# Even output projection of a two-layer trunk: eight products of halves against seven

## What is computed

```python
def even_layer(x, norm_g, w_in, conv_w, pool_w, pool_scale, w_out):
    h = rmsnorm(x, norm_g)
    xa, bg, cg, gate_a, u, gate_b = split_cols(h @ w_in, EVEN_SIZES)      # six parts of 512
    ya = short_conv_mixer(xa, bg, cg, conv_w) * jax.nn.silu(gate_a)
    yb = pool_mixer(u, pool_w, pool_scale) * jax.nn.silu(gate_b)
    return x + jnp.concatenate([ya, yb], axis=-1) @ w_out                # 1024 x 1024
```

## Time and profile before

| | |
|---|---|
| median of three runs | 1697.89 us (1697.84 to 1700.63) |
| profiled execution, its own time | 1699.45 us |
| profiled execution, its span | 1697.6 us |
| TensorE busy | 1673.1 us, 8096 matmuls |
| VectorE, ScalarE, GpSimd busy | 765.5, 483.3, 335.7 us |
| DMA over the span | 342.69 MB, mean 202 GB/s |

### The profile page before, as it was taken

One profiled execution on the slowest core, in us unless ns is written; L12 is line 12 of the kernel. 1 busy time (PEld: TensorE's weight loads), 2 busy tenths in 40 slices (PEclk: granted clock), 3 DMA queues, 4 the chain that ended last, 5 costly groups with the idle time before them and its releaser, 6 DMA issues.

```text
span 1697.6 us, 21999 instructions
## 1 busy us (share of the span) xinstructions
PE 1673.1 (99%) x8096; PEld 1391.4 (82%) x8096; DVE 765.5 (45%) x1328; ACT 483.3 (28%) x1153; POOL 335.7 (20%) x463
## 2 busy tenths in 40 slices
PE   8999999999999999999999999999999999999998
PEld 7887788888788788888888888888888888888886
DVE  3645335675422432566432333357544232245742
ACT  2000223562200023365310002437431000243731
POOL 8777674447400000000110000000001000000000
PEclk9999999999999999999999999999999999999999
DMA  8887687658855545544676555644467555554444
GB/s 270 308 292 263 217 287 237 208 182 286 310 195 191 179 168 195 166 134 140 229 256 198 187 183 177 194 141 137 145 228 265 192 189 183 186 172 141 136 161 149
DMA packets 162323, 342.69 MB, mean 202 GB/s; under 512 B 32128, under 2 KB 83840, under 8 KB 162208
## 3 DMA queue, kind: packets, MB, share of 16 engines
q1 hardware_dynamic: 139520, 313.57, 55.2%
q10 hardware_dynamic: 22688, 27.64, 5.2%
HBM read 263.50 MB, written 77.66 MB: 201 GB/s over the span
## 4 chain that ended last, share of the span: by engine, by line
PE 91%; DVE 3%; POOL 2%; ACT 1%; DMA 1%; issue 1%; ACTq 0%; POOLq 0%; DVEq 0%; SPq 0%
PE bank L478 14%; PE bank L480 14%; PE bank L479 14%; PE pair_a L478 5%; PE pair_a L480 5%; PE pair_a L479 5%; PE pair_b L478 4%; PE pair_c L478 4%; PE pair_c L480 4%; PE pair_c L479 4%; PE pair_b L480 4%; PE pair_b L479 4%; PE pair_a L773 2%; PE pair_c L756 2%; PE pair_b L670 1%; POOL slot L428 1%
## 5 line engine op out<-in xcount | busy, mean ns | idle before, releaser
L478 PE MATMUL bank<-h_hi,slot 128*128 128x512 f32 (+1 forms) x976 | 381.3, 391 | 5.1 <-POOL slot L428 2.1
L480 PE MATMUL bank<-h_hi,slot 128*128 128x512 f32 (+1 forms) x976 | 377.7, 387 | 0.0
L479 PE MATMUL bank<-h_lo,slot 128*128 128x512 f32 (+1 forms) x976 | 377.2, 387 | 0.0
L403 POOL TENSOR_TENSOR rs<-sums,eps 128x1 f32<-128x1 f32 x48 | 10.0, 207 | 1064.0 <-ACT junk L853 1064.0
L478 PEld LDWEIGHTS bank<-h_hi,slot 128*128 128x128 f32 x976 | 183.8, 188 | 43.6 <-POOL slot L428 2.3
L480 PEld LDWEIGHTS bank<-h_hi,slot 128*128 128x128 f32 x976 | 183.8, 188 | 37.8
L479 PEld LDWEIGHTS bank<-h_lo,slot 128*128 128x128 f32 x976 | 183.9, 188 | 37.2 <-issue 1.0
L428 POOL TENSOR_TENSOR slot<-stages,slot 128x512 fp32r<-128x512 f32 x132 | 180.6, 1368 | 11.0
L426 POOL TENSOR_SCALAR slot<-stages 128x512 fp32r<-128x512 f32 x132 | 93.2, 706 | 122.1 <-issue 104.5
L478 PE MATMUL pair_a<-h_hi,slot 128*128 128x512 f32 x256 | 101.3, 396 | 0.0
L480 PE MATMUL pair_a<-h_hi,slot 128*128 128x512 f32 x256 | 99.6, 389 | 0.0
(11 more groups left out here) (287 smaller groups left out, 3175.5 us busy)
## 6 DMA issues: line engine op xcount, KB each, us to landing
slot<-split_weights SPq DMA_DIRECT2D x396, 512.0 KB, 3.4
split_weights<-slot SPq DMA_DIRECT2D x132, 512.0 KB, 4.1
stages<-in_even_w_in SPq DMA_DIRECT2D x48, 256.0 KB, 3.8
stages<-in_odd_w_in SPq DMA_DIRECT2D x36, 256.0 KB, 3.2
result<-res ACTq DMA_DIRECT2D x16, 512.0 KB, 5.6
xin<-in_x ACTq DMA_DIRECT2D x12, 512.0 KB, 7.5
stages<-in_even_w_out SPq DMA_DIRECT2D x16, 256.0 KB, 3.2
stages<-in_odd_w_in SPq DMA_DIRECT2D x32, 128.0 KB, 2.8
```

The source lines that it names most:

```text
L478: t.matmul(dst, l_hi, r_hi, start=start, stop=False)
L479: t.matmul(dst, l_hi, r_lo, start=False, stop=False)
L480: return t.matmul(dst, l_lo, r_hi, start=False, stop=stop)
```

## The change

In blocks two to four (b = 1 to 3) the projection Y W (Y: 512 tokens x 1024, W: 1024 x 1024) is computed from halves. Y is cut by tokens (early, late: 256 each) and by rows of y (the convolution part and the pooling part, 512 each); W by rows and columns. Seven products of such halves take the place of eight. Four of them take sums of weight halves, three take stored halves; four take sums of y halves.

* PE: `seven_products` in place of the old order (now `plain_projection`, kept for block one). A product has four k-slices, each on one half unit and two token tiles: 6 matmuls. Order: P1, P2, P5, P6, P3, P4, the transposes of tile 0, P7 tile by tile with the transposes of tile 1 between, then the values. A block reads 28 half units there in place of 16 (`EXTRA` = 12).
* DVE: in blocks two to four the convolution's y stays in `res`; only the early half of it is split. After each `pool_end` four linked operations make the sums of y. The low parts of the sums (`sum_lo`) and 22 additions of 128x512 in place of 8 follow.
* ACT: high parts of the sums, and copies of the two banks of P1.
* GpSimd, in block two only: `combine(k)` makes four sums of weight slices and splits them in high and low. SP loads the raw slices, stores the results in `combined_weights` and reads them like other half units.
* The blocks two and three are written out on PE and SP instead of looped; on ACT and DVE block one now stands apart from the loop.

```diff
+HALVES1 = HALVES + EXTRA
+PRODUCTS = P1, P2, P5, P6, P3, P4, P7 = range(7)
+SUM1, SUM2, SUM4, SUM3 = range(4)
+ODD_BANK = (2, 0, 2, 0)
...
+            def save_combined(n):
+                sp.wait_ge(s_comb_split, n + 1)
+                sp.dma_start(combined_dram[n % 4, n // 4], combined[n % 2].bitcast(F32)).then_inc(s_comb_saved[n % 2], 16)
+                if n + 4 < 16:
+                    load_raw(n % 4, n // 4 + 1)
...
+            for place in range(4):
+                load_raw(place, 0)
+            for b in range(1, NB):
+                for i in range(HALVES1):
+                    if b == 1 and i >= 4 and i % 2 == 0 and i < 36:
+                        save_combined((i - 4) // 2)
+                    if b == 1 and i == 40:
+                        for place in range(2):
+                            sp.wait_ge(s_comb_saved[place], 16 * 8)
+                    if b < NB - 1 or i + SLOTS < HALVES1:
+                        sp.wait_ge(s_half, b * HALVES1 - EXTRA + i + 1)
+                        load_half((i + SLOTS) % HALVES1)
...
+            def combine(k):
...
+                g.tensor_tensor(stage[T1], stage[T3], stage[T1], ALU.subtract).then_inc(s_combined, 1)
...
+                for place in range(4):
+                    m = n + place
+                    if m >= 2:
+                        pool.wait_ge(s_comb_saved[m % 2], 16 * (m // 2))
+                    c_hi, c_lo = combined[m % 2][:, 0:HALF], combined[m % 2][:, HALF:2 * HALF]
+                    g.tensor_scalar(c_hi, stage[place], 1.0, 0.0, ALU.mult, ALU.add).then_inc(s_comb_hi, 1)
+                    pool.wait_ge(s_comb_hi, m + 1)
+                    g.tensor_tensor(c_lo, stage[place], c_hi.bitcast(F32), ALU.subtract).then_inc(s_comb_split, 1)
...
+                def seven_products():
+
+                    pe.wait_ge(s_pool_gate, b * 4 + 3)
+                    for k in range(4):
+                        product_of_y(P1, 0, 0, 0, k)
+                        if k == 0:
+                            pool_product(3)
+                    for k in range(4):
+                        if k == 0:
+                            pe.wait_ge(s_ye, b * 8 + 6)
+                        elif k >= 2:
+                            pe.wait_ge(s_ye, b * 8 + 4 + k + 1)
+                        product_of_y(P2, 4, 0, 4, k)
+                    product_of_sum(P5, SUM1, 6)
+                    pe.wait_ge(s_pool_gate, b * 4 + 4)
+                    product_of_sum(P6, SUM2, 2)
+                    pe.wait_ge(s_res, b * 8 + 2)
+                    product_of_sum(P3, SUM4, 4)
+                    pe.wait_ge(s_twelve, (b - 1) * 4 + 2)
+                    for k in range(4):
+                        product_of_y(P4, 4, 2 * P, 0, k)
+                    pe.wait_ge(s_res, b * 8 + 4)
+                    transposes(tile(0), 0, first_bank=ODD_BANK[0])
...
+                    for kp, tt in ((0, 0), (0, 1), (1, 0), (1, 1), (0, 2), (1, 2), (0, 3), (1, 3)):
+                        if kp == 0:
+                            pe.wait_ge(s_hlo, 2 * tile(tt) + 2)
+                        value_part(kp, tt)
+                        if tt == 1:
+                            if kp == 0:
+                                pe.wait_ge(s_res, b * 8 + 8)
+                            else:
+                                pe.wait_ge(s_hlo, 2 * tile(1) + 2)
+                            transposes(tile(kp + 2), kp + 2, first_bank=ODD_BANK[kp + 2])
...
+                    if not opening_block(b):
+                        early, late = y[:, 0:2 * P], y[:, 2 * P:TB]
+                        a11, a21, sum1, sum2 = [sums4[:, g, i, :] for i in range(4)]
+                        link(v.tensor_tensor(sum1, a21, late, ALU.add))
+                        link(v.tensor_tensor(sum2, sum1, a11, ALU.subtract))
+                        link(v.tensor_tensor(a11, a11, a21, ALU.subtract))
+                        v.tensor_tensor(a21, early, sum2, ALU.subtract).then_inc(s_sums, 1)
                     split_y(4 + g, y, s_ye)
```

More of the change, by code:

```diff
@@ L51 @@
 HALVES = 2 * UNITS
+EXTRA = 12
+HALVES1 = HALVES + EXTRA
 STAGES = 5
@@ L134, in trunk @@
         work = sb("work", [P, 8 * TB])
+        sums4 = res[:, :, :].rearrange("p k (s t) -> p k s t", s=4)
+        total = [work[:, 2048 + 512 * i:2560 + 512 * i] for i in range(2)]
         q_att = [y_hi, y_lo]
@@ L140, in trunk @@
         keys = sb("keys", [P, 2, KVH, KW], F32R)
+        combined = [keys[:, :, :, :].rearrange("p a g w -> p (a g w)")[:, 2 * HALF * i:2 * HALF * (i + 1)]
+                    for i in range(2)]
         k_hh = [keys[:, 0, g, :] for g in range(KVH)]
@@ L224, in trunk @@
         s_slot = [sem(f"slot_loaded{i}") for i in range(SLOTS)]
+        s_raw = [sem(f"raw_weights{i}") for i in range(4)]
+        s_combined = sem("weights_combined")
+        s_comb_hi = sem("combined_hi")
+        s_comb_split = sem("combined_split")
+        s_comb_saved = [sem(f"combined_saved{i}") for i in range(2)]
+        s_sums = sem("sums_of_y")
+        s_sum_step = sem("sum_step")
+        s_sum_hi = sem("sum_hi")
+        s_sum_lo = sem("sum_lo")
+        s_part = sem("partial_residual")
+        s_first_product = sem("first_product_copied")
+        s_twelve = sem("products_summed")
+        s_seven = sem("first_tile_of_p7")
         s_x = [sem(f"x_in{i}") for i in range(TT)]
@@ L332, in load_half, with load_raw @@
             def load_half(i):
-                sp.dma_start(slots[i % SLOTS][:, :].bitcast(F32), split_dram[i]).then_inc(s_slot[i % SLOTS], 16)
+                sp.dma_start(slots[i % SLOTS][:, :].bitcast(F32), later[i]).then_inc(s_slot[i % SLOTS], 16)
+            def load_raw(place, k):
+                col = {T1: 0, T3: HALF, T2: HALF, T4: 0}[place]
+                row = P * k + (HALF if place in (T2, T4) else 0)
+                sp.dma_start(stage[place], ewo[row:row + P, col:col + HALF]).then_inc(s_raw[place], 16)
+            def save_combined(n):
[3 more added lines that the diff above has]
+                    load_raw(n % 4, n // 4 + 1)
             x_rows = x[0]
@@ L601, in tile @@
                     return b * 8 + TT + tt
[L603 to L623, removed]
@@ L638, in body, with product_part, product_of_y @@
                             last.then_inc(s_half, 1)
-                    if kp == 0 and tt < 2:
-                        odd_transposes(tt + 2)
+                def product_part(p, k, t2, src_hi, src_lo, row, col, dst):
+                    sl, a = (2 * U_EOUT + 4 * p + k) % SLOTS, slice(col + t2 * P, col + (t2 + 1) * P)
+                    return mm3(banks[dst + t2], src_hi[:, row, a], src_lo[:, row, a], w_hi[sl], w_lo[sl],
+                               k == 0, k == 3)
+                def product_of_y(p, rows, col, dst, k):
+                    slot(2 * U_EOUT + 4 * p + k)
+                    for t2 in range(2):
+                        last = product_part(p, k, t2, y_hi, y_lo, rows + k, col, dst)
+                    last.then_inc(s_half, 1)
@@ L821, in _ @@
             body(0, True, False)
-            with pe.Fori(1, NB - 1) as b:
+            for b in range(1, NB - 1):
                 body(b, False, False)
```

314 lines of the change are left out of this document (248 added, 66 removed).

## The result

The change makes the kernel slightly slower: a median of 1702.1 us against 1698.0 us over 20 runs each, ratio 1.0022 (95% interval 1.0015 to 1.0028). The forecast was 1682.6 us. A second set of runs beside the last experiments gives 1703.8 against 1699.1 us, ratio 1.0025 (1.0014 to 1.0036).

What follows compares the result with a forecast made beforehand. TensorE was taken as the bound, busy 1673.1 of 1697.6 us. 72 fewer matmuls (-16.3 us) plus 1.0 for transposes gave -15.3: 1684.1 us against the profiled execution, 1682.6 us as median; 8 in 10 range 1681 to 1690.

Steps and rivals of the forecast that it cites:

- The stages: Projections of blocks two to four: 24 matmuls fewer each at 0.227 us, 16.3 us less in all.
- The weight traffic: Projection stages: 28 loads in place of 16, 512 KB every 1.36 us, 385 GB/s demanded; cost 0 us.
- The rival of late loads in the stage: The 28 loads of each of three stages land late, up to 9.9 us: +18 us, 1716 us; chance 7%.
- Row groups 5 and 6: Earlier trace rows for weight traffic: 408 to 416 GB/s with full queues; loads landing in 3.1 to 3.5 us in the stage.
- The chain of y and its sums: DVE after each pool end: four linked 128x256 operations, 1.65 us, done 2.7 us before PE wants them; 0 us.
- The transposes of tile 2: After P7, PE waits 0.6 us for DVE where it waited 0.28: +0.3 us a block, +1.0 us over three.
- Block two alone: GpSimd's weight sums and SP's raw loads and stores in block two: 0 us, at worst a few us once.
- SP is held up in block two: Rival: GpSimd's rounds 4 us longer hold SP's queue, PE waits 3 to 5 us once, 1687 us; chance 7%.
- catches up: Block two: SP, about 6 us late, recovers within a round, 21 us of work against 8 halves, 21.8 us.
- 3 us to spare: Opening of block two, where loads land in 5.8 to 9.9 us: ordinary loads still 3 us ahead of need.
- The range: Whole kernel: 8 in 10 range of the forecast time, 1681 to 1690 us.
- the held queue: Block two: SP's wait for GpSimd delays the ordinary loads behind it; forecast as a rival at 1687 us, chance 7%.

Runs made afterwards that it cites:

- experiment 3: The change with GpSimd issuing the 16 raw loads and 16 stores on its own queue: 1681.4 us, ratio 0.9899; again 1682.9 us, 0.9898.
- Experiment 7: The change with SP's ordinary load issued before the wait for GpSimd, store and raw load at 16 places: 1698.6 us, ratio 0.9998.
- experiment 5: The change without the 16 stores and 12 later raw loads; GpSimd's arithmetic and SP's 16 waits stay: 1683.5 us, ratio 0.9901.

## Why the prediction was wrong

**The stages were right.** 24 matmuls fewer at 0.227 us, less the longer wait for DVE, made 5.1 us in blocks three and four. In block two it was 5.8, since the kernel before took 0.7 us more there than in its next block (415.9 against 415.2). The weight traffic came as costed, over the windows of the products of block three of the change:

```profile
1014.00:1044.00 30.00, 30.00 (x138) 24.94 (x137) 19.32 (x28) 7.91 (x15) 2.69 (x6) 1.00 0.96 364
```

A DMA share of 0.96 (0.95 forecast), 364 GB/s (370 to 390), landing times of 3.3 / 4.8 / 5.3 us as minimum, median and maximum (3.3 to 5), under the 6.8 us at which it would begin to cost. PE is busy 30.00 of 30.00 us. The rival of late loads in the stage, 7%, did not happen, and the 358 GB/s of the Trainium skill ("DMA: Bandwidth & Descriptors", "Where 436 GB/s comes from") did not bind this single core: the change moved 364 GB/s over 30 us and 405 over 6.7. Row groups 5 and 6 were the right ones to go by.

**The chain of y and its sums was right.** Its rows in block three are as costed from the earlier trace rows, 0.42 us a link:

```profile
1011.01 0.42 DVE L1429 TENSOR_TENSOR res<-res,work 128x256 f32<-128x256 f32 x1
1011.47 0.42 DVE L1430 TENSOR_TENSOR res<-res 128x256 f32<-128x256 f32 x1
...
1016.75 0.69 DVE L1374 TENSOR_TENSOR y_lo<-proj,y_hi 128x512 fp32r<-128x512 f32 x1
1017.51 3.50 DVE L1473 TENSOR_TENSOR h_lo<-res,h_hi 128x1024 fp32r<-128x1024 f32 x3
```

**The transposes of tile 2** wait 0.7 us in every block (0.6 forecast), at the place named:

```profile
1054.04 1.06 PE L588 MATMUL pair_a<-ident,work 128*128 128x128 f32 x8 [0.68 <-DVE work L1312]
```

**The step that failed is "Block two alone", costed at 0 us; it cost 20.8.** The mechanism stood there, SP's wait ahead of ordinary loads, and as a rival at 7%, "SP is held up in block two". With the queue free (experiment 3) the kernel took 1681.4 and 1682.9 us, so the rest of the sum, 1682.6, held. Four terms of the step were mis-sized.
First, the landing of a raw slice inside the round: I took 3.2 us from the earlier trace rows, a median over block one. Here it is 3.8 / 8.2 / 13.3 us (minimum, median, maximum). The share of the engines doesn't explain this: it was 0.79 over 132 to 178 us, where those 16 loads of block one were made, and 0.78 in the change over 445 to 575 us. What differs is that the slice is asked for right behind a 512 KB store; on GpSimd's queue, where this was so too, it took 6.3 / 7.7 / 11.1 us. No run took the store away from the load, so this cause isn't shown. The stores land in 6.8 us at the median, not 4.1. With 13.3 us of arithmetic, 8.1 us of waiting for slices and 5.3 us for stores, and small gaps, a round is 27.4 us and not 21.
Second, "catches up": I compared 6 us of delay with 10 us of slack as if every round began anew. A round longer than its schedule adds its excess each time: 5.6 us a round over three rounds is 16.8, behind a first store that was already 12 us late. The slack was smaller too, since ordinary loads landed in 7.8 us at the median and not in 3.4. Experiment 7 fell to the same mistake.
Third, the rival's price, 3 to 5 us once, left out the clock, which fell at two of the waits: 5.7 us of the 20.8.
Fourth, the opening: "3 us to spare" went by landings of up to 9.9 us, and the load behind the raw slices took 15.8, which made the wait of 2.5 us at 461 us.
The range, 1681 to 1690, held this rival only at its price of 1687. The forecast's own sum of a round, 13.8 us of arithmetic, 3.2 for a slice and 4.1 for a store, is 21.1 us; with the median landing of the earlier trace rows, 6.8 us, in both places it is 27.4, an estimate from rows at hand before the change that meets the measured round, and it would have made the held queue the main rival.

## What to carry to other kernels

A wait placed in a queue that also feeds the bottleneck must be costed with the whole loop behind it: arithmetic plus every landing, at landing times under the new load, against the time that the schedule gives a round. If the round is longer, the excess adds up from round to round, and the slack of a ring is spent only once; give it more room in the schedule, take a landing out of the round by asking earlier, or move it to a queue on which nothing else depends. Here each of the three brought back nearly the whole gain of 1%, and the arithmetic alone (experiment 5) had cost next to nothing.

## What the runs showed of the hardware

At a wait of TensorE of several us the granted clock fell to 0.50, 1.2 GHz, where it had stood at 2.4 GHz: at the waits of 4.5 and 5.5 us for stretches of 6.8 us in the change, which began 0.7 and 1.1 us before the wait ended. It is not one price for one length: the change's own waits of 2.5 us at 461 and 526 us left the clock alone, while in its second profile a wait of 2.0 us at 461 us and each of the later ones, 2.7 to 3.9 us, went with 3.4 us at half clock. The four stretches of that profile lose 6.6 us beside 12.1 us of waits; for the shortest wait the loss, 1.6 us, is nearly as much again as the wait itself. GpSimd's own queue landed its 512 KB stores in 6.8 us at the median, with the engines at a share of 0.90 over 445 to 555 us; SP's took 6.8 us in the change as well, at 0.78.
